# GpSimd's quarter of the low weights from the eleventh z unit on, in place of from the fourth xbc unit on

## The chip, the core and the metric

One NeuronCore of a Trainium2 chip runs the whole program. Five engines work beside each other and meet only at semaphores: TensorE (PE, with its weight loads shown as PEld), VectorE (DVE), ScalarE (ACT), GpSimd (POOL) and SyncE (SP), which here only issues DMAs. The metric is the device time of one execution in microseconds (us), less is better. The kernel before takes 1279.44 us (median of 3 runs, 1279.43 to 1281.62).

## The reference

Two decoder layers on 256 tokens of width 1024, all in float32. Each layer is a half-weighted SwiGLU, a token mixer, a cross attention to 256 memory tokens and a second SwiGLU. The mixer of layer 0 is a short gated convolution, that of layer 1 is a Mamba-2 mixer (SSD). The change lies in the SSD mixer:

```python
z, xbc, dt = jnp.split(h @ w_in, [D_INNER, D_INNER + SSD_CONV_DIM], axis=-1)   # 2048, 4096, 32 columns
xbc = jax.nn.silu(_causal_depthwise_conv(xbc, conv_kernel) + conv_bias)
xs, bm, cm = jnp.split(xbc, [D_INNER, D_INNER + SSD_GROUPS * D_STATE], axis=-1)
dt = jax.nn.softplus(dt + dt_bias);  da = dt * -jnp.exp(a_log);  a_cum = jnp.cumsum(da, axis=-1)
decay = _segsum_exp(a_cum)              # exp(a_cum[l] - a_cum[s]) for s <= l: 32 heads x 2 chunks x 128 x 128
y_diag = jnp.einsum("bgcls,bgrcls,bcsgrp->bclgrp", cb, decay, xdt)
```

followed by the carried state, the gate silu(z), a norm by group and the output projection.

## The kernel before, in words

Every float32 product is made of three products of reduced parts. A weight tile is cut into `w_hi`, its value rounded to the fast matmul type, and `w_lo`, the rest; activations likewise.

The weights stream through four slots, one unit of 128x1024 values at a time, and the units are numbered through the whole program: the SSD mixer has one dt unit, 16 z units, 32 xbc units and 16 half units of the output projection. In this text z0 to z15 and xbc0 to xbc31 are these units, so z10 is the eleventh z unit and xbc3 the fourth xbc unit. For each unit

- SP loads it into `raw` (L339), once `w_lo` of the unit four places earlier is made (L336);
- ACT rounds it into `w_hi` (L422, in the profile line L413);
- DVE subtracts: `w_lo = raw - w_hi` (L850, in the profile line L835), and counts `lo_ready`;
- PE multiplies with both. A z unit is twelve matmuls of 512 columns in two halves (`wide_unit`, L1718), where the first half (k = 0) reads columns 0 to 511 of the unit and the second (k = 1) the rest. An xbc unit is 24 matmuls of 256 columns (`unit`, L1468).

For the units in `SHARED` (L311), which is xbc3 to xbc31, DVE makes only the first 768 columns of `w_lo`, and GpSimd the last 256 (L1413), counted by `lo_pool`. PE waits for both counts, and SP for both before it loads the slot again (L338).

The order of each engine is written out by hand. In step s of the z stage (s = 0 to 15) ACT and DVE split unit z(s+3), three units ahead of PE. Between these splits they have other work:

- `normed`: the normalised activations for the xbc stage, eight tiles of 128x256. DVE multiplies two tiles a step in steps 4 to 7 (L1215), ACT rounds one a step in steps 5 to 12 (L656), GpSimd subtracts one behind each (L1407).
- `decay`: from step 7 to step 14 DVE subtracts and clips eight blocks of 128x128 a step (`diffs`, L1184), and ACT takes the exponential a step later in two instructions of 128x512 (L644). The blocks come by eight broadcast DMAs of 512 KB (L373), which SP issues between the loads of the last z units.
- after the last exponential ACT evicts the last z tiles (`evict_z(3)`, L687), and then rounds xbc3 (L694).

In the xbc stage DVE has three multiply-adds of a convolution out of PSUM for each unit.

Of the kernel before, what the change touches and what calls it, by code (L numbers as in the profile page):

```python
# [19 lines left out]
F32 = mybir.dt.float32  # L20
F32R = mybir.dt.float32r
ALU = mybir.AluOpType
# [6 lines left out]
KT = D_MODEL // P  # L29
# [5 lines left out]
GROUPS = 8  # L35
# [9 lines left out]
UNIT_W = KT * P  # L45
DOWN_W = FT // 2 * P
SLOTS = 4
AHEAD = 3
# [43 lines left out]
def trunk(nc, x_t, mem_t, small, w_gu, w_down, w_conv_in, w_conv_out, w_z, w_xbc, w_dt, w_ssd_out,  # L92
          w_q, w_k, w_v, w_o, out_t, rows_d):
    first, uses, n_units = plan()
# [4 lines left out]
    with ExitStack() as ctx:  # L99
# [19 lines left out]
        a_hi, a_lo, a_lo_at = a[:, 0], a[:, 1], a_hi_at + 4 * FT * SEQ  # L119
        raw = sb("raw", [P, SLOTS, DOWN_W])  # L120
        w_hi, w_hi_at = zip(*(sb_at(f"w_hi{s}", [P, DOWN_W], F32R) for s in range(SLOTS)))
        w_lo, w_lo_at = zip(*(sb_at(f"w_lo{s}", [P, DOWN_W], F32R) for s in range(SLOTS)))
# [4 lines left out]
        z = nc.alloc_sbuf_tensor_at("z", [P, 2, D_INNER], F32, offset=mark + (-mark) % 32)  # L127
# [44 lines left out]
        normed = [t[:, i] for t in (t1_all, t2_all, gate_all, xd) for i in range(2)]  # L172
# [25 lines left out]
        hi_ready, lo_ready = sem("hi_ready"), sem("lo_ready")  # L198
# [24 lines left out]
        normed_ready, nhi_ready, nh_ready = sem("normed_ready"), sem("nhi_ready"), sem("nh_ready")  # L223
        conv_begun, xbc_ready, y_added = (sem(n) for n in ("conv_begun", "xbc_ready", "y_added"))
        lo_pool = sem("lo_pool")
# [71 lines left out]
        H_NORMED = 8  # L297
# [10 lines left out]
        LATE, LAST_ROOT = 5, 7  # L308
        MEM_AGAIN = 36
        SHARED_W = UNIT_W - 256  # L310
        SHARED = range(first["xbc"] + AHEAD, first["xbc"] + 4 * GROUPS)  # L311
        TAIL = {"y": {7: 35}, "zs": {7: 36}, "state": {7: 36}, "y_add": {7: 36}, "yo": {6: 34, 7: 36}, "yoff": {6: 35, 7: 37},
                "square": {6: 36, 7: 38}, "root": {6: 37, 7: 38}, "yn": {5: 35, 6: 37, 7: 38}, "yt": {5: 35, 6: 38, 7: 39}, "a_rest": {5: 36, 6: 39, 7: 40}}
        STEADY = {"cb": 4, "xt": 5, "b_nat": 5, "m0": 5, "m1": 6, "xn": 6, "y": 9, "zs": 9, "state": 10, "y_add": 10, "yo": 11,
# [1022 lines left out]
        @block.gpsimd  # L1337
        def _(pool):
            steps = [0]
            chain = [0]  # L1340

            def add_squares(b):

                for k in range(1, adds(b) + 1):
                    pool.wait_ge(sq_ready, KT * b + k + 1)
                    if k > 1:
                        pool.wait_ge(ssq_step, adds_ahead(b) + k - 1)
                    first_term = sq[0] if k == 1 else ssq
                    nc.gpsimd.tensor_tensor(ssq[:, :], first_term[:, :], sq[k % 3][:, :], ALU.add).then_inc(ssq_step, 1)  # L1349

            def mem_square(i):

                pool.wait_ge(mem_step, 2 * i)
                src = mem[:, bass.ds(i - 1, 1), :].rearrange("p a n -> p (a n)")
                nc.gpsimd.tensor_tensor(mem_sq[:, :], src, src, ALU.mult).then_inc(mem_step, 1)
                pool.wait_ge(mem_step, 2 * i + 1)
                nc.gpsimd.tensor_tensor(mem_ssq[:, :], mem_ssq[:, :], mem_sq[:, :], ALU.add).then_inc(mem_step, 1)

            def a_part(j, count, src):
                pool.wait_ge(ahi_ready, count + 1)  # L1360
                nc.gpsimd.tensor_tensor(j(a_lo), src, j(a_hi).bitcast(F32), ALU.subtract).then_inc(a_ready, 1)  # L1361

            def ffn(f):
                for j in range(2):
                    a_part(lambda t, j=j: t[:, j, :], FFN_A[f] + j, t2[j][:, :])
                if f == 0:
                    pool.wait_ge(mem_in, 64)
                    nc.gpsimd.memset(mem_ssq[:, :], 0.0).then_inc(mem_step, 1)
                    nc.gpsimd.memset(mem_sq[:, :], 0.0).then_inc(mem_step, 1)
                for lo, hi in ((1, KT + 1), (KT + 1, FT // 2)):  # L1370
                    with pool.Fori(lo, hi) as i:
                        for q in range(2):
                            a_part(lambda t, q=q: t[:, bass.ds(2 * i + q, 1), :].rearrange("p a n -> p (a n)"),
                                   FFN_A[f] + 2 * i + q, t2[q][:, :])
                        if f == 0 and lo == 1:
                            mem_square(i)
                project_out(f"down{f}")

            def project_out(phase):
                add_squares(OUT_NORM[phase])  # L1380

            def attention(layer):
                for k in range(KT):
                    a_part(lambda t, k=k: t[:, KT + k, :], Q_A[layer] + k, t2[k % 2][:, :])
                project_out(f"o{layer}")

            def inverse_root_y(g):

                def step(ins, done=pool_step):
                    ins.then_inc(done, 1)  # L1390
                    if done is pool_step:
                        chain[0] += 1
                        pool.wait_ge(pool_step, chain[0])
                r, v, w = (t[:, g % 2, :] for t in (rms_y, var_y, root_y))
                step(nc.gpsimd.tensor_scalar(v, sum_y[:, g % 2, :], 1.0 / GW, EPS, ALU.mult, ALU.add))
                step(nc.gpsimd.tensor_scalar(r.bitcast(mybir.dt.int32), v.bitcast(mybir.dt.int32), -0.5, float(0x5f3759df), ALU.mult, ALU.add))
                for i in range(3):
                    step(nc.gpsimd.tensor_tensor(w, v, r, ALU.mult))
                    step(nc.gpsimd.tensor_tensor(w, w, r, ALU.mult))
                    step(nc.gpsimd.tensor_scalar(w, w, -0.5, 1.5, ALU.mult, ALU.add))  # L1400
                    step(nc.gpsimd.tensor_tensor(r, w, r, ALU.mult), rmsy_ready if i == 2 else pool_step)

            def ssd():
                nx = first["xbc"]
                for k in range(KT):
                    pool.wait_ge(nhi_ready, k + 1)
                    nc.gpsimd.tensor_tensor(a_lo[:, H_NORMED + k, :], normed[k], a_hi[:, H_NORMED + k, :].bitcast(F32), ALU.subtract).then_inc(nh_ready, 1)  # L1407
                for t in range(SSD_STEPS):
                    if nx + t + AHEAD in SHARED:
                        n = nx + t + AHEAD  # L1410
                        s = n % SLOTS
                        pool.wait_ge(hi_ready, n + 1)
                        nc.gpsimd.tensor_tensor(w_lo[s][:, SHARED_W:UNIT_W], raw[:, s, SHARED_W:UNIT_W],  # L1413
                                                w_hi[s][:, SHARED_W:UNIT_W].bitcast(F32), ALU.subtract).then_inc(lo_pool, 1)
                    if ("yoff", t) in due and due["yoff", t] < LATE:
                        g = due["yoff", t]
                        pool.wait_ge(yoff_ready, g + 1)
                        pool.wait_ge(y_added, g + 1)
                        nc.gpsimd.tensor_tensor(y[g % 2][:, 1, :], y[g % 2][:, 1, :], y_off, ALU.add).then_inc(ysum_ready, 1)
                        pool.wait_ge(ysum_ready, g + 1)  # L1420
                        pool.wait_ge(zs_ready, g + 1)
                        nc.gpsimd.tensor_tensor(y[g % 2][:, :, :], y[g % 2][:, :, :], zs[:, :, :], ALU.mult).then_inc(y_ready, 1)
                    if ("root", t) in due and due["root", t] < LAST_ROOT:
                        g = due["root", t]
                        pool.wait_ge(ysq_ready, 2 * g + 2)
                        at_least(pool, yn_ready, 2 * (g - 1))
                        inverse_root_y(g)
                project_out("ssd_out")

            add_squares(0)  # L1430
            ffn(0)
            for k in range(KT):
                a_part(lambda t, k=k: t[:, k, :], CONV_A + k, t2[k % 2][:, :])
            project_out("conv_out")
            attention(0)
            ffn(1)
            ffn(2)
            ssd()
            attention(1)
            ffn(3)  # L1440
# [3 lines left out]
        def _(pe):  # L1444
# [273 lines left out]
            def wide_unit(n, outs, k0, l_hi, l_lo, start, stop, ready=None, part=range(2)):  # L1718

                s = n % SLOTS  # L1720
                pe.wait_ge(lo_ready, n + 1)
                for k in part:
                    if ready:
                        pe.wait_ge(ready[0], ready[1] + k0 + k + 1)
                    w = slice(k * 512, k * 512 + 512)
                    for t in range(2):
                        lt = slice(t * P, t * P + P)
                        ins = three(outs[t][:, :], l_hi[:, k0 + k, lt], l_lo[:, k0 + k, lt], w_hi[s][:, w], w_lo[s][:, w],
                                    start and k == 0, stop and k == 1)
                if k == 1:  # L1730
                    ins.then_inc(unit_done, 1)
# [213 lines left out]
```

## Time and profile before

| | |
|---|---|
| median of 3 runs | 1279.44 us (1279.43 to 1281.62) |
| the profiled execution | 1279.97 us, its span 1278.2 us |
| PE busy | 1268.3 us, 99% of the span |
| DVE busy | 991.9 us, 78% |
| ACT busy | 765.8 us, 60% |
| POOL busy | 261.2 us, 20% |
| granted TensorE clock | 0.999 of full speed |

Times inside the program are microseconds from the start of the span. "Busy" counts the time in which an engine has an instruction in work. In the timelines, neighbouring instructions of one kind are merged, with their number behind x; the bracket at a row's end is the idle time of the engine ahead of it and what ended it. The last z units, the decays and the first xbc units lie between 786 and 829 us.

### The profile page before, as it was taken

What the parts mean: (1) busy time and instruction counts of PE and PEld (TensorE: products, weight loads), DVE (VectorE), ACT (ScalarE), POOL (GpSimd) and SP (SyncE); (2) the same over time, 40 slices, a digit from 0 to 9 for tenths busy, and PEclk for the clock granted to TensorE, in tenths of its full rate; (3) what the DMA queues carried; (4) which work ended last, traced back from release to release, by engine and by line L of the source; (5) the groups of instructions that cost most, each with busy time, mean ns of one, the idle gap of its engine ahead of it and who ended that gap; (6) DMA issues with size and microseconds to landing.
All of it is one profiled execution on the core that took longest, in us unless ns stands there. A gap on an engine that the chain in (4) does not pass through costs nothing.

```text
span 1278.2 us, 23174 instructions
## 1 busy us (share of the span) xinstructions
PE 1268.3 (99%) x7882; PEld 1143.7 (89%) x7882; DVE 991.9 (78%) x1573; ACT 765.8 (60%) x1402; POOL 261.2 (20%) x339
## 2 busy tenths in 40 slices
PE   9999999999999999999999999999999999999997
PEld 7888888898899888888888888999999889888887
DVE  6877778897868787768778768989988777787754
ACT  6655654555655556545656456878866656556643
POOL 2433110123001111111111112336521201111111
PEclk9999999999999999999999999999999999999999
DMA  8566645555545556654556647744445554555661
GB/s 281 174 196 196 223 158 171 197 189 169 165 133 181 188 188 203 223 163 158 193 190 213 213 148 260 228 156 143 134 158 173 182 166 143 170 184 193 220 211 47
DMA packets 63093, 232.49 MB, mean 182 GB/s; under 512 B 7024, under 2 KB 8112, under 8 KB 62896
## 3 DMA queue, kind: packets, MB, share of 16 engines
q1 hardware_dynamic: 62224, 229.69, 55.1%
q10 hardware_dynamic: 800, 1.91, 0.4%
q8 instruction: 40, 0.66, 0.2%
q14 instruction: 29, 0.24, 0.1%
HBM read 230.49 MB, written 1.08 MB: 181 GB/s over the span
## 4 chain that ended last, share of the span: by engine, by line
PE 96%; DMA 1%; DVE 1%; ACT 0%; issue 0%; ACTq 0%; DVEq 0%
PE bank L1446 95%; DMA raw<-w_z 1%; DVE w_lo L835 1%; DMA raw<-w_gu 0%; ACT w_hi L413 0%; PE bank L1801 0%; PE bank L1829 0%; PE bank L1638 0%; DVE decay L1184 0%; PE bank L1576 0%; PE bank L1856 0%; DVE t L838 0%; DVE final L1334 0%; PE bank L1787 0%; ACT L680 0%
## 5 line engine op out<-in xcount | busy, mean ns | idle before, releaser
L835 DVE TENSOR_TENSOR w_lo<-raw,w_hi 128x1024 fp32r<-128x1024 f32 (+3 forms) x403 | 520.1, 1293 | 28.7 <-ACT w_hi L413 28.3
L413 ACT ACTIVATE w_hi<-raw 128x1024 fp32r<-128x1024 f32 (+2 forms) x403 | 442.0, 1098 | 90.1 <-PE bank L1446 80.8
L1446 PE MATMUL bank<-h,w_hi 128*128 128x512 f32 x1744 | 425.7, 391 | 1.4 <-DVE h L838 1.3
L1446 PE MATMUL bank<-a,w_hi 128*128 128x256 f32 (+1 forms) x1878 | 381.6, 324 | 0.4 <-DVE w_lo L835 0.2
L1446 PEld LDWEIGHTS bank<-h,w_hi 128*128 128x128 f32 x1744 | 317.7, 188 | 62.0 <-DVE h L838 2.1
L1446 PEld LDWEIGHTS bank<-a,w_hi 128*128 128x128 f32 x1878 | 312.5, 190 | 26.3 <-issue 0.5
L1446 PE MATMUL bank<-a,w_lo 128*128 128x256 f32 x1280 | 256.4, 283 | 0.0
L1446 PEld LDWEIGHTS bank<-h,w_lo 128*128 128x128 f32 x1736 | 228.5, 191 | 11.2
L1446 PE MATMUL bank<-h,w_lo 128*128 128x256 f32 x1736 | 233.7, 282 | 0.0
L413 ACT ACTIVATE corr<-bank 128x256 f32<-128x256 f32 x263 | 99.0, 377 | 208.3 <-PE bank L1446 208.1
L1446 PEld LDWEIGHTS bank<-a,w_lo 128*128 128x128 f32 x1280 | 201.0, 191 | 2.7
L1361 POOL TENSOR_TENSOR a<-t,a 128x256 f32 (+1 forms) x112 | 102.0, 911 | 492.4 <-ACT a L413 492.4
L835 DVE TENSOR_TENSOR t<-bank,corr 128x256 f32<-128x256 f32 x207 | 86.6, 419 | 88.1 <-ACT corr L413 81.4
L1349 POOL TENSOR_TENSOR ssq<-ssq,sq 128x256 f32<-128x256 f32 x51 | 51.1, 1003 | 181.6 <-ACT sq L446 180.9
L835 DVE TENSOR_TENSOR t<-t,rms 128x256 f32<-128x256 f32 x88 | 72.7, 826 | 3.1
L413 ACT ACTIVATE a<-t 128x256 f32 (+1 forms) x116 | 47.5, 411 | 37.0 <-DVE t L835 37.0
L413 ACT ACTIVATE h<-x,cst 128x256 fp32r<-128x256 f32 x64 | 32.2, 508 | 60.9 <-DVE x L835 60.3
L835 DVE TENSOR_TENSOR acc<-bank,corr 128x256 f32<-128x256 f32 x32 | 13.6, 424 | 67.6 <-ACT corr L413 67.6
L838 DVE SCALAR_TENSOR_TENSOR h<-x,cst,h 128x256 fp32r<-128x256 f32 x64 | 51.3, 806 | 8.0 <-ACT h L413 8.0
L1349 POOL TENSOR_TENSOR ssq<-sq 128x256 f32<-128x256 f32 x9 | 10.2, 1135 | 212.3 <-ACT sq L446 212.3
L838 DVE SCALAR_TENSOR_TENSOR acc<-bank,cst,acc 128x253 f32<-128x253 f32 (+2 forms) x96 | 45.9, 479 | 6.5 <-ACT acc L704 3.8
L835 DVE TENSOR_TENSOR t<-t,gate 128x256 f32<-128x256 f32 (+1 forms) x89 | 38.4, 431 | 10.9 <-ACT gate L466 1.9
(201 smaller groups left out, 1037.6 us busy)
## 6 DMA issues: line engine op xcount, KB each, us to landing
raw<-w_gu SPq DMA_DIRECT2D x174, 512.0 KB, 3.6
raw<-w_down SPq DMA_DIRECT2D x64, 704.0 KB, 4.3
raw<-w_xbc SPq DMA_DIRECT2D x32, 512.0 KB, 4.3
raw<-w_conv_in SPq DMA_DIRECT2D x24, 512.0 KB, 3.5
raw<-w_q SPq DMA_DIRECT2D x16, 512.0 KB, 3.8
raw<-w_k SPq DMA_DIRECT2D x16, 512.0 KB, 3.4
raw<-w_v SPq DMA_DIRECT2D x16, 512.0 KB, 3.5
raw<-w_o SPq DMA_DIRECT2D x16, 512.0 KB, 4.0
```

The costliest lines, as they stand in the source:

```text
L413: return nc.scalar.activation(out, in_, ACT.Copy, scale=scale)
L835: return nc.vector.tensor_tensor(out, a, b, op)
L838: return nc.vector.scalar_tensor_tensor(out=out, in0=a, scalar=scalar, in1=b, op0=op0, op1=op1)
L1349: nc.gpsimd.tensor_tensor(ssq[:, :], first_term[:, :], sq[k % 3][:, :], ALU.add).then_inc(ssq_step, 1)
L1361: nc.gpsimd.tensor_tensor(j(a_lo), src, j(a_hi).bitcast(F32), ALU.subtract).then_inc(a_ready, 1)
L1446: return nc.tensor.matmul(out, lhs, rhs, start=start, stop=stop, skip_group_check=check)
```

## The change

The range `SHARED` begins nine units earlier, at z10: GpSimd now makes columns 768 to 1023 of `w_lo` for z10 to z15 and xbc0 to xbc2 as well, and DVE only columns 0 to 767 of these. GpSimd's code puts the part of unit z(s+3) ahead of its `normed` subtraction of step s. PE waits for `lo_pool` in a shared z unit ahead of the second half only, and in xbc0 to xbc2 ahead of the unit; SP waits for `lo_pool` too before it loads the units four places behind these nine.

```diff
@@ -308,7 +308,8 @@
         SHARED_W = UNIT_W - 256
-        SHARED = range(first["xbc"] + AHEAD, first["xbc"] + 4 * GROUPS)
+        Z_SHARED = 10
+        SHARED = range(first["z"] + Z_SHARED, first["xbc"] + 4 * GROUPS)
@@ -1384,6 +1385,13 @@
+            def low_part(n):
+
+                s = n % SLOTS
+                pool.wait_ge(hi_ready, n + 1)
+                nc.gpsimd.tensor_tensor(w_lo[s][:, SHARED_W:UNIT_W], raw[:, s, SHARED_W:UNIT_W],
+                                        w_hi[s][:, SHARED_W:UNIT_W].bitcast(F32), ALU.subtract).then_inc(lo_pool, 1)
@@ -1401,17 +1409,17 @@
             def ssd():
-                nx = first["xbc"]
-                for k in range(KT):
-                    pool.wait_ge(nhi_ready, k + 1)
-                    nc.gpsimd.tensor_tensor(a_lo[:, H_NORMED + k, :], normed[k], a_hi[:, H_NORMED + k, :].bitcast(F32), ALU.subtract).then_inc(nh_ready, 1)
+                nz, nx = first["z"], first["xbc"]
+                for s in range(5, 16):
+                    if nz + s + AHEAD in SHARED:
+                        low_part(nz + s + AHEAD)
+                    if s < 5 + KT:
+                        k = s - 5
+                        pool.wait_ge(nhi_ready, k + 1)
+                        nc.gpsimd.tensor_tensor(a_lo[:, H_NORMED + k, :], normed[k], a_hi[:, H_NORMED + k, :].bitcast(F32), ALU.subtract).then_inc(nh_ready, 1)
                 for t in range(SSD_STEPS):
                     if nx + t + AHEAD in SHARED:
-                        n = nx + t + AHEAD
-                        s = n % SLOTS
-                        pool.wait_ge(hi_ready, n + 1)
-                        nc.gpsimd.tensor_tensor(w_lo[s][:, SHARED_W:UNIT_W], raw[:, s, SHARED_W:UNIT_W],
-                                                w_hi[s][:, SHARED_W:UNIT_W].bitcast(F32), ALU.subtract).then_inc(lo_pool, 1)
+                        low_part(nx + t + AHEAD)
@@ -1722,6 +1730,8 @@
                 for k in part:
                     if ready:
                         pe.wait_ge(ready[0], ready[1] + k0 + k + 1)
+                    if n in SHARED and k == 1:
+                        pe.wait_ge(lo_pool, n - SHARED[0] + 1)
```

GpSimd's instructions at the start of the SSD mixer, before the change: the eight `normed` subtractions (`a<-t,a`, `a<-gate,a`, `a<-xd,a`), then the shared parts.

```order
L1407 TENSOR_TENSOR a<-t,a 128x256 [waits nhi_ready] x4
L1407 TENSOR_TENSOR a<-gate,a 128x256 [waits nhi_ready] x2
L1407 TENSOR_TENSOR a<-xd,a 128x256 [waits nhi_ready] x2
L1413 TENSOR_TENSOR w_lo<-raw,w_hi 128x256 [waits hi_ready] x13
```

And after the change, at the same place (the code's lines are up to twelve further down):

```order
L1419 TENSOR_TENSOR a<-t,a 128x256 [waits nhi_ready] x2
L1392 TENSOR_TENSOR w_lo<-raw,w_hi 128x256 [waits hi_ready]
L1419 TENSOR_TENSOR a<-t,a 128x256 [waits nhi_ready]
L1392 TENSOR_TENSOR w_lo<-raw,w_hi 128x256 [waits hi_ready]
L1419 TENSOR_TENSOR a<-t,a 128x256 [waits nhi_ready]
L1392 TENSOR_TENSOR w_lo<-raw,w_hi 128x256 [waits hi_ready]
L1419 TENSOR_TENSOR a<-gate,a 128x256 [waits nhi_ready]
L1392 TENSOR_TENSOR w_lo<-raw,w_hi 128x256 [waits hi_ready]
L1419 TENSOR_TENSOR a<-gate,a 128x256 [waits nhi_ready]
L1392 TENSOR_TENSOR w_lo<-raw,w_hi 128x256 [waits hi_ready]
L1419 TENSOR_TENSOR a<-xd,a 128x256 [waits nhi_ready]
L1392 TENSOR_TENSOR w_lo<-raw,w_hi 128x256 [waits hi_ready]
```

Six parts of z10 to z15 now stand between the `normed` subtractions from the third on; those of xbc0 to xbc2 follow behind the last.

PE in the middle of a late z unit, before the change:

```order
L1446 MATMUL bank<-w_hi,h 128x512 [waits lo_ready]
L1446 MATMUL bank<-w_lo,h 128x512
L1446 MATMUL bank<-w_hi,h 128x512 x2
L1446 MATMUL bank<-w_lo,h 128x512
L1446 MATMUL bank<-w_hi,h 128x512 x2
L1446 MATMUL bank<-w_lo,h 128x512
```

and after it, z10:

```order
L1454 MATMUL bank<-w_hi,h 128x512 [waits lo_ready]
L1454 MATMUL bank<-w_lo,h 128x512
L1454 MATMUL bank<-w_hi,h 128x512 x2
L1454 MATMUL bank<-w_lo,h 128x512
L1454 MATMUL bank<-w_hi,h 128x512
L1454 MATMUL bank<-w_hi,h 128x512 [waits lo_pool]
L1454 MATMUL bank<-w_lo,h 128x512
```

The matmuls are the same; the seventh of the unit, the first that reads columns from 512 on, has the wait for GpSimd's part.

## Rows read from the trace of the kernel before

**Rows 1.** The profile's page: busy time, share of the span and instructions.

```profile
PE 1268.3 (99%) x7882; PEld 1143.7 (89%) x7882; DVE 991.9 (78%) x1573; ACT 765.8 (60%) x1402; POOL 261.2 (20%) x339
```

**Rows 2.** Waits of PE's weight loads, 765 to 830 us: total, times, longest.

```profile
PEld bank L1446 <- DVE w_lo L835: 0.7, 1, 0.7
PEld bank L1446 <- issue: 0.5, 1, 0.5
```

**Rows 3.** Timeline of PE: start, length (us), what, count, idle before.

```profile
802.41 0.39 PE L1446 MATMUL bank<-w_hi,h 128*128 128x512 f32 x1
803.03 0.50 PE L1446 MATMUL bank<-w_hi,h 128*128 128x512 f32 x1 [0.24 <-DVE w_lo L835]
...
808.45 0.39 PE L1446 MATMUL bank<-w_hi,h 128*128 128x512 f32 x1
808.98 0.48 PE L1446 MATMUL bank<-a,w_hi 128*128 128x256 f32 x2
...
817.69 0.45 PE L1446 MATMUL bank<-a,w_hi 128*128 128x256 f32 x2
```

**Rows 4.** Timeline of DVE from z10's low part on.

```profile
784.54 0.87 DVE L838 SCALAR_TENSOR_TENSOR gate<-x,cst,rms 128x256 f32<-128x256 f32 x2
787.01 1.23 DVE L835 TENSOR_TENSOR w_lo<-raw,w_hi 128x1024 fp32r<-128x1024 f32 x1 [1.59 <-ACT w_hi L413]
788.15 1.36 DVE L838 SCALAR_TENSOR_TENSOR xd<-x,cst,rms 128x256 f32<-128x256 f32 x2
...
792.14 2.14 DVE L1184 TENSOR_SCALAR decay<-decay,dt_nacum 128x128 f32<-128x128 f32 x8
...
797.97 1.22 DVE L835 TENSOR_TENSOR w_lo<-raw,w_hi 128x1024 fp32r<-128x1024 f32 x1 [0.51 <-ACT w_hi L413]
799.12 2.73 DVE L1184 TENSOR_SCALAR decay<-decay,dt_nacum 128x128 f32<-128x128 f32 x8
...
811.50 1.66 DVE L1184 TENSOR_SCALAR decay<-decay,dt_nacum 128x128 f32<-128x128 f32 x8
813.07 1.21 DVE L835 TENSOR_TENSOR w_lo<-raw,w_hi 128x1024 fp32r<-128x1024 f32 x1
815.96 0.96 DVE L835 TENSOR_TENSOR w_lo<-raw,w_hi 128x768 fp32r<-128x768 f32 x1 [1.67 <-ACT w_hi L413]
816.83 1.51 DVE L838 SCALAR_TENSOR_TENSOR acc<-bank,cst,acc 128x253 f32<-128x253 f32 x3
...
822.00 2.93 DVE L838 SCALAR_TENSOR_TENSOR acc<-bank,cst,acc 128x253 f32<-128x253 f32 x6
```

**Rows 5.** Timeline of POOL over the same stretch.

```profile
791.55 1.27 POOL L1407 TENSOR_TENSOR a<-t,a 128x256 fp32r<-128x256 f32 x1 [2.71 <-ACT a L413]
...
798.33 1.47 POOL L1407 TENSOR_TENSOR a<-gate,a 128x256 fp32r<-128x256 f32 x1 [2.32 <-ACT a L413]
800.96 0.80 POOL L1407 TENSOR_TENSOR a<-xd,a 128x256 fp32r<-128x256 f32 x1 [1.16 <-ACT a L413]
...
816.00 2.21 POOL L1413 TENSOR_TENSOR w_lo<-raw,w_hi 128x256 fp32r<-128x256 f32 x2 [9.72 <-ACT w_hi L413]
...
822.24 0.74 POOL L1413 TENSOR_TENSOR w_lo<-raw,w_hi 128x256 fp32r<-128x256 f32 x1 [0.97 <-ACT w_hi L413]
```

**Rows 6.** Timeline of ACT at the end of the decays.

```profile
813.19 0.64 ACT L644 ACTIVATE decay<-decay 128x512 f32<-128x512 f32 x1 [0.15 <-DVE decay L1184]
813.73 1.25 ACT L413 ACTIVATE z<-bank,rms_n 128x512 f32<-128x512 f32 x2
814.86 1.06 ACT L413 ACTIVATE w_hi<-raw 128x1024 fp32r<-128x1024 f32 x1
```

**Rows 7.** DVE groups from 788 to 815 us: count, busy, mean ns.

```profile
L1184 DVE TENSOR_SCALAR decay<-decay,dt_nacum 128x128 f32<-128x128 f32 x64 | 15.7, 316 | 0.0
```

**Rows 8.** Busy time of each engine in a window, clock, DMA share, GB/s.

```profile
core 0: us, PE busy (x) PEld busy (x) DVE busy (x) ACT busy (x) POOL busy (x), PEclk, DMA share, GB/s
787.00:813.00 26.00, 25.62 (x127) 21.24 (x126) 25.48 (x74) 20.66 (x33) 8.17 (x6) 1.00 0.90 319
```

## What the change does to the time: the prediction

> **What bounds the kernel now.** I read the page's busy shares first, then the waits of PE in the stretch of the change, then the timelines of PE, DVE, POOL and ACT there. PE is busy in 1268.3 of 1278.2 us [rows 1], so what PE does not wait for is worth nothing, and a wait that PE gets is paid in full: no later stage has PE slack in which to lose it. From 765 to 830 us PE's weight loads wait for a low part in two places, 0.7 and 0.5 us [rows 2]; the second is named "issue", but it starts as the first low part of xbc ends. On PE's timeline the loss is smaller. Matmuls of 512 columns normally start 0.23 us apart (a z unit of twelve is 2.75 us), and here the starts are 802.41 and 803.03 us (z14 is late by 0.39) and 808.45 and 808.98 us (xbc0 is late by 0.30) [rows 3]. The most that earlier low parts can give back is 0.69 us.
>
> Both waits are for DVE. In 787 to 813 us it is busy 25.48 of 26 us [rows 8], with one gap of 0.51 us at 797.97 [rows 4]. So the question is whether DVE gets through this stretch sooner, not how much GpSimd could carry (8.17 us busy there).
>
> **What DVE is relieved of.** Where it works without a break, a low part of 1024 columns takes 1.14 us of DVE (787.01 to the next start at 788.15) and one of 768 takes 0.87 (815.96 to 816.83) [rows 4]. Nine units save 0.27 each. Up to the last decay (the start of xbc2's low part, 813.07) eight of them count: 2.16 us.
>
> **What it is charged.** GpSimd gets nine subtractions of 128x256 float32, of the same shape as the eight that it has there. What each of these does to DVE shows in rows 4 and 5. Eight decay subtractions with no GpSimd operation beside them take 1.57 us to the next start (811.50 to 813.07, row length 1.66). The eight at 792.14 have a row of 2.14: GpSimd's operation that began at 791.55 was waiting as DVE's low part ended, went first, and DVE stood for 0.49. The eight at 799.12 have 2.73: two GpSimd operations (798.33 and 800.96), 1.07 together, so the one that began among the decays cost about 0.59. The products at 788.15 take 1.36 against 0.87 at 784.54: 0.49 again. GpSimd pays too: 1.27 and 1.47 us for an operation that takes 0.74 alone (822.24) [rows 5].
>
> Not all DVE work is held up. At 822.00 six multiply-adds that read PSUM take 2.93 us, against 1.51 for three, with a GpSimd part from 822.24 to 822.98 beside them and nothing lost [rows 4, 5]. There the 29 shared parts of before are cheap, since DVE's other work in that stage is of this kind. In the z stage the other work is the decays, from SBUF to SBUF.
>
> So a shared part there takes 0.27 us off DVE and puts 0.49 to 0.59 on. I take 0.54, the middle of the two kinds of meeting. The bounds are 0 (all meet idle time or PSUM work, as at 822.24) and 0.74 (DVE stands for GpSimd's whole operation).
>
> The Trainium skill (SBUF — State Buffer, section Who interferes with whom, with the bullets of SBUF: two separate sides) says that VectorE and GpSimd arbitrate for one port pair by an exclusive lock held for the whole instruction, and that the loser fully blocks. The trace agrees that one of them stands, but prices it at 0.49 to 0.59 and not at the 0.74 of the whole row.
>
> **The sum.** DVE from 787.01 to 813.07 before: eight low parts 9.1; two products 0.87; 64 decays [rows 7], eight times 1.57, 12.6; GpSimd 3.0 (five meetings of 0.49, one of 0.59); the gap 0.51. That is 26.1 and the stretch is 26.06. After: eight low parts 8 x 0.87 = 6.96; products 0.87; decays 12.6; the old meetings 3.0; nine new ones (z10 to z15, xbc0, xbc1, and xbc2, whose `w_hi` is rounded while the last decays run) 9 x 0.54 = 4.86; no gap, since with DVE later z13's `w_hi` is there. That is 28.3, so xbc2's low part starts 2.2 us later, at 815.3.
>
> PE sees it thus. With two GpSimd operations in it, the shared part and a `normed` one, a step costs DVE 0.87 + 1.57 + 0.49 + 0.54 = 3.5 us, while PE is through a z unit in 2.75; in xbc0 and xbc1, with one, it is 2.98 against PE's 2.88 (24 matmuls 0.12 apart). Laid out step by step from 787.01, DVE is ahead of PE up to z12, level at z13, and from z14 on PE waits unit by unit, some 1 us behind today at z14 and 1.5 at xbc0 and xbc1. These are one lag, not several. The last step of it is a chain that today ends in time by less than 0.1 us: last decays (813.07), their exponential on ACT (813.19), the eviction of the last z tiles (813.73), `w_hi` of xbc3 (814.86 to 815.92) [rows 6], its low part on DVE (815.96) and on GpSimd (two parts from 816.00 take 2.21, the second 0.74 of it, so the first is done by about 817.5), PE at 817.69 [rows 3 to 5]. Shifted by 2.2, less the little slack, PE starts xbc3 2.1 us later. PE's two losses of before are inside this number, as it compares places in the span. Behind xbc3 DVE, ACT and PE stand to each other as today, and nothing gives the 2.1 back.
>
> **The waits added.** PE's new wait stands at the seventh matmul of a shared z unit, with the rest of the unit behind it. It ends before PE comes to it: GpSimd begins as soon as `w_hi` is there, while DVE still has decays to do, so `lo_ready`, 1.4 us earlier in PE's order, is last: nothing. On GpSimd the queue behind a shared part is one `normed` subtraction, which PE reads from 809 us on; xbc0 starts at about 810.5 by then and reads the last tile 2.5 us later, when GpSimd is long past it. SP's loads behind z10 to z15 come later with DVE by 0.3 to 1 us. DMA runs at 0.90 of its share in 787 to 813 us [rows 8], so what waits in its queue is not all delayed, and the `w_hi` of z14 to xbc2 have a microsecond between landing and need once DVE is late. Nothing again; if the cover fails it is up to 1 us more.
>
> The profiled execution took 1279.97 us: with 2.1 it would take 1282.1. It lies 0.5 above the median of the runs, 1279.44; on that the forecast is 1281.5.
>
> **The rivals.**
>
> *GpSimd holds DVE longer, or the lag spreads.* At 0.74 a meeting: 9 x 0.74 - 2.16 - 0.51 = 4.0 us, 1283.4. Late slot loads in the full DMA queue would come to about the same. For it: new pairs of GpSimd operations follow each other closely, which today happens once. Against: no meeting in the trace costs over 0.59. The Trainium skill's rule of a block for the whole instruction (SBUF — State Buffer, Who interferes with whom), read by the row's length, is this case.
>
> *The meetings are cheaper.* GpSimd may fall into DVE's idle time ahead of a low part, as at 816.00, where DVE's 768 columns keep their 0.96 and DVE then goes to PSUM work. If a part costs 0.3 to 0.4, DVE is late by 0 to 0.9: 1279.4 to 1280.4. For it: z10 to z12 have real idle time ahead of them (1.59 us at 787.01). Against: from 788 on DVE has work from SBUF without a break, and each meeting there cost 0.49 or more.
>
> *The other side: faster.* DVE comes through sooner, and PE's 0.39 and 0.30 vanish: 1278.8. It decides at a cost of (2.16 + 0.51) / 9 = 0.30 us per shared part; below that the last decay is not later than today. For it: the same sharing is in use from xbc3 on with PE not waiting. Against: that stage has no decays.
>
> That the change does not do what it says is not a case; the instruction order has it.
>
> **How the numbers follow.** A measurement of this kernel can tell 0.2%, 2.6 us, from no change. Forecast (own range +1.3 to +2.8, 1280.7 to 1282.3): 0.60. Longer holds or a spread lag: 0.15. Cheaper meetings: 0.17. Faster: 0.08. Over +2.6 us is a quarter of the first case and nearly all of the second: 0.28. Under -2.6 us there is no mechanism, PE having only 0.69 to win: 0.02. The rest, 0.70, is within 0.2%. For 8 in 10 I leave out most of the faster case and the upper half of the second, and allow for runs that scatter from 1279.4 to 1281.6: 1279.1 to 1283.6.
>
> **What would show it.** Decay rows of eight with 2.6 to 2.8 us where today they have 1.65 to 2.14; `w_lo` of 768 columns, yet xbc2's low part at about 815.3; PE waiting for `w_lo` on nearly each unit from z14 to xbc3; xbc3 at about 819.8 on PE; the same matmuls behind it at a constant distance of 2 us from today. I am wrong if the decay rows keep their length, if PE's waits are for `lo_pool`, or if PE is ahead of today at xbc3.

## The result, and the profile after

The changed kernel takes 1282.38 us, the median of 15 runs (from 1281.67 us), beside 1279.63 us (1279.17 to 1281.62, 15 runs) for the kernel before. The ratio is 1.0021, with a 95% interval of 1.0014 to 1.0028: slower by 2.7 us, between 1.8 and 3.6. One execution of the changed kernel took 2539.88 us, for a reason that no trace shows; ratio and interval leave it out. The profiled execution took 1281.72 us, span 1279.9, against 1279.97 and 1278.2 before: 1.75 us more.

The page's busy line of the changed kernel answers to [rows 1].

```profile
PE 1269.1 (99%) x7882; PEld 1143.8 (89%) x7882; DVE 993.5 (78%) x1573; ACT 766.7 (60%) x1402; POOL 268.5 (21%) x348
```

GpSimd has nine instructions more. DVE, which was relieved of 9 x 256 columns, is busy for 1.6 us longer, not shorter.

The waits of PE's weight loads from 765 to 830 us (answers to [rows 2]):

```profile
PEld bank L1454 <- DVE w_lo L836: 1.3, 2, 0.9
PEld bank L1454 <- issue: 1.1, 2, 0.8
PEld bank L1454 <- ACT z L414: 0.4, 1, 0.4
```

Where there were two waits of 1.2 us in all, there are five of 2.8 (a wait of 0.4 for `corr` is in both and left out here), and one of them is of a kind that was not there: for ACT's eviction of a z tile. None is put down to GpSimd; but the later of the two named "issue", 0.26 us at xbc3, ends as GpSimd's part of xbc3 does (see below).

PE's timeline at the places of [rows 3], and xbc2: the rows are z14, xbc0, xbc2 and xbc3.

```profile
803.38 0.50 PE L1454 MATMUL bank<-w_hi,h 128*128 128x512 f32 x1 [0.46 <-DVE w_lo L836]
...
809.84 0.48 PE L1454 MATMUL bank<-a,w_hi 128*128 128x256 f32 x2 [0.44 <-issue]
...
816.16 0.50 PE L1454 MATMUL bank<-a,w_hi 128*128 128x256 f32 x2 [0.21 <-ACT z L414]
...
819.37 0.48 PE L1454 MATMUL bank<-a,w_hi 128*128 128x256 f32 x2
```

And xbc2 in the kernel before:

```profile
814.81 0.40 PE L1446 MATMUL bank<-a,w_hi 128*128 128x256 f32 x2
```

z14 starts at 803.38 (803.03 before), xbc0 at 809.84 (808.98), xbc2 at 816.16 (814.81), xbc3 at 819.37 (817.69). The lateness grows over the stretch, 0.35, 0.86, 1.35 and at last 1.68 us.

DVE from z10's low part to xbc2's, whole (answers to [rows 4]):

```profile
786.92 0.96 DVE L836 TENSOR_TENSOR w_lo<-raw,w_hi 128x768 fp32r<-128x768 f32 x1 [1.41 <-ACT w_hi L414]
787.80 1.84 DVE L839 SCALAR_TENSOR_TENSOR xd<-x,cst,rms 128x256 f32<-128x256 f32 x2
789.56 2.14 DVE L1185 TENSOR_SCALAR decay<-decay,dt_nacum 128x128 f32<-128x128 f32 x8
791.62 0.95 DVE L836 TENSOR_TENSOR w_lo<-raw,w_hi 128x768 fp32r<-128x768 f32 x1
792.49 3.12 DVE L1185 TENSOR_SCALAR decay<-decay,dt_nacum 128x128 f32<-128x128 f32 x8
795.53 0.95 DVE L836 TENSOR_TENSOR w_lo<-raw,w_hi 128x768 fp32r<-128x768 f32 x1
796.40 1.65 DVE L1185 TENSOR_SCALAR decay<-decay,dt_nacum 128x128 f32<-128x128 f32 x8
797.97 0.94 DVE L836 TENSOR_TENSOR w_lo<-raw,w_hi 128x768 fp32r<-128x768 f32 x1
798.84 3.62 DVE L1185 TENSOR_SCALAR decay<-decay,dt_nacum 128x128 f32<-128x128 f32 x8
802.38 0.95 DVE L836 TENSOR_TENSOR w_lo<-raw,w_hi 128x768 fp32r<-128x768 f32 x1
803.24 2.22 DVE L1185 TENSOR_SCALAR decay<-decay,dt_nacum 128x128 f32<-128x128 f32 x8
805.38 0.95 DVE L836 TENSOR_TENSOR w_lo<-raw,w_hi 128x768 fp32r<-128x768 f32 x1
806.25 2.62 DVE L1185 TENSOR_SCALAR decay<-decay,dt_nacum 128x128 f32<-128x128 f32 x8
808.79 0.95 DVE L836 TENSOR_TENSOR w_lo<-raw,w_hi 128x768 fp32r<-128x768 f32 x1
809.66 2.21 DVE L1185 TENSOR_SCALAR decay<-decay,dt_nacum 128x128 f32<-128x128 f32 x8
811.79 0.95 DVE L836 TENSOR_TENSOR w_lo<-raw,w_hi 128x768 fp32r<-128x768 f32 x1
812.66 2.21 DVE L1185 TENSOR_SCALAR decay<-decay,dt_nacum 128x128 f32<-128x128 f32 x8
814.78 0.95 DVE L836 TENSOR_TENSOR w_lo<-raw,w_hi 128x768 fp32r<-128x768 f32 x1
```

The rows of eight decays are a measure of what GpSimd does to DVE: 1.65 us alone, 2.14 to 2.22 with one GpSimd operation beside them, 2.62 with two, 3.12 with three, 3.62 with four. The four at 798.84 are on GpSimd's own timeline (answers to [rows 5]):

```profile
797.85 1.67 POOL L1392 TENSOR_TENSOR w_lo<-raw,w_hi 128x256 fp32r<-128x256 f32 x1 [2.32 <-ACT w_hi L414]
799.47 0.74 POOL L1419 TENSOR_TENSOR a<-gate,a 128x256 fp32r<-128x256 f32 x1
800.48 0.81 POOL L1392 TENSOR_TENSOR w_lo<-raw,w_hi 128x256 fp32r<-128x256 f32 x1 [0.27 <-ACT w_hi L414]
801.25 0.73 POOL L1419 TENSOR_TENSOR a<-xd,a 128x256 fp32r<-128x256 f32 x1
...
817.71 2.21 POOL L1392 TENSOR_TENSOR w_lo<-raw,w_hi 128x256 fp32r<-128x256 f32 x2 [3.32 <-ACT w_hi L414]
```

The first of them began 0.12 us ahead of DVE's low part of 797.97, stood until that had ended (1.67 instead of 0.74) and then went first. So the engines do not meet only at semaphores, as the first section has it: DVE and GpSimd also stand for each other while both work from SBUF.

The same 64 decays as one group (787 to 816 us; answers to [rows 7]), and the window of [rows 8] with its columns:

```profile
L1185 DVE TENSOR_SCALAR decay<-decay,dt_nacum 128x128 f32<-128x128 f32 x64 | 19.8, 379 | 0.0
```

```profile
787.00:813.00 26.00, 25.10 (x120) 20.32 (x119) 26.00 (x68) 19.55 (x32) 13.57 (x14) 1.00 0.86 318
```

The decays take 19.8 us where they took 15.7. In 787 to 813 us DVE has no idle time at all (26.00 of 26) and ends six instructions behind (68 for 74), PE seven behind (120 for 127). The granted clock is full, as before.

ACT behind the last decay (answers to [rows 6]):

```profile
814.90 0.63 ACT L645 ACTIVATE decay<-decay 128x512 f32<-128x512 f32 x1 [0.71 <-DVE decay L1185]
815.43 1.25 ACT L414 ACTIVATE z<-bank,rms_n 128x512 f32<-128x512 f32 x2
```

and the pieces of the chain that ended last, in order of time (start, us, what):

```profile
812.74 2.14 DVE decay L1185 x8
...
814.90 0.03 ACT decay L645
...
815.43 0.68 ACT z L414
...
816.16 3.13 PE bank L1454 x24
```

The last decays let ACT begin their exponential; the eviction of the last z tiles stands in ACT's queue behind it, and frees the bank that xbc2's matmuls write. From 786.92 to 814.87 the chain is DVE's alone. Behind the 24 matmuls of xbc2 PE stands once more: the first of GpSimd's two parts from 817.71 (2.21 us in all, the second 0.74 of it) ends at about 819.2, and xbc3 starts at 819.37. The kernel before has this wait in its code too, but there the part ends in time.

### The profile page after: what moved, and what is told of

It is laid out like the page before. It is cut to its first block, busy times and chain, and to the rows that moved or that the text cites. A ratio compares the mean times of both kernels' runs of the same rounds, so it can differ in the third digit from the quotient of the medians.

```text
span 1279.9 us, 23193 instructions
## 1 busy us (share of the span) xinstructions
PE 1269.1 (99%) x7882; PEld 1143.8 (89%) x7882; DVE 993.5 (78%) x1573; ACT 766.7 (60%) x1402; POOL 268.5 (21%) x348
## 4 chain that ended last, share of the span: by engine, by line
PE 95%; DVE 3%; DMA 1%; ACT 0%; issue 0%; ACTq 0%; DVEq 0%; SPq 0%
PE bank L1454 94%; DVE decay L1185 1%; DVE w_lo L836 1%; DMA raw<-w_z 0%; DMA raw<-w_gu 0%; PE bank L1811 0%; PE bank L1839 0%; PE bank L1646 0%; ACT w_hi L414 0%; PE bank L1584 0%; DVE xd L839 0%; PE bank L1866 0%; DMA rows_d<-rows 0%; DVE final L1335 0%; PE bank L1797 0%
## 5 line engine op out<-in xcount | busy, mean ns | idle before, releaser
L1350 POOL TENSOR_TENSOR ssq<-sq 128x256 f32<-128x256 f32 x9 | 10.2, 1133 | 212.6 <-ACT sq L447 212.6
```

## The experiments

**How they are compared.** The whole time scatters by more than the effects (see the last section), so each trace is also read over places in it: the distance on PE from the first matmul of z10 to those of z14, xbc0 and xbc3, and from xbc3 to the last matmul; and on DVE from the start of z10's low part to that of xbc2's. "Ops" is the number of full-width GpSimd subtractions in DVE's stretch. The last column is a sum: the stretch, less its gaps, less 8 low parts (1.14 us each of 1024 columns, 0.87 of 768), 0.87 for the products and 8 x 1.57 for the decays, over the ops. Medians are of timed runs, "one" is a single run; the kernel before stood at 1279.63 beside `after`, 1280.28 beside the first four experiments and 1279.84 beside the next four.

```
trace          median   ratio [95%]               PE z10 to z14, xbc0, xbc3  rest    DVE    gaps  ops  per op
before         1279.63                            11.28  17.23  25.93        453.75  26.06  0.51   6   0.50
before_again   one 1281.86                        10.88  16.58  25.28        453.79  25.55  0      6   0.50
before_third   one 1279.72                        10.88  16.72  25.42        453.74  25.67  0.13   6   0.50
e7             1280.35  1.0006 [0.9997, 1.0015]   10.88  16.72  25.42        453.94  25.67  0.03   6   0.51
after          1282.38  1.0021 [1.0014, 1.0028]   11.51  17.96  27.50        453.81  27.86  0     15   0.50
after_again    1282.49  1.0020 [1.0011, 1.0029]   11.75  18.20  27.73        453.80  27.92  0     15   0.50
after_third    one 1284.41                        11.85  18.30  27.84        453.78  27.91  0     15   0.50
e1             1279.50  0.9990 [0.9981, 0.9999]   10.88  16.74  25.45        453.75  25.23  1.68   6   0.53
e2             1284.49  1.0029 [1.0018, 1.0041]   13.33  20.35  30.22        453.74  30.40  0     15   0.52
e3             1282.09  1.0013 [1.0004, 1.0022]   11.57  17.97  27.51        453.82  27.63  0.40  12   0.50
e4             1281.37  1.0006 [0.9997, 1.0015]   11.40  17.56  27.05        453.85  27.38  0.83   9   0.50
e5             1279.63  0.9998 [0.9989, 1.0007]   10.88  16.32  24.95        453.75  25.03  0.52   4   0.49
e6             1281.81  1.0014 [1.0005, 1.0023]   11.40  18.00  27.19        453.76  27.31  0.28  13   0.51
```

The theory: in this stretch each GpSimd subtraction stops DVE's work between two SBUF tiles for about half a microsecond, twice what 256 columns are worth to it, and PE gets the difference as lateness. The rivals: the added waits and their places, later loads, a cost that hangs on GpSimd's work anywhere.

**The pair again.** No edit: after_again, before_again and after_third, before_third are the two kernels once more.

> The changed kernel once more, beside the kernels of this call. In the one trace PE is 1.62 us later behind xbc3 and 0.02 us later anywhere ahead of z14, while the medians lie 2.75 apart. Theory: the path has only those 1.6 us, and the rest is scatter of single runs (1281.67 to 1284.51): a ratio of 1.0013 to 1.0020, and again all of the shift between z14 and xbc3. Rival (a second cost that the first trace missed, as late loads in some executions): a shift in the trace away from that stretch, and again 2.7 us.

> The kernel before once more, for its trace alone. In the run with nine more operations in the xbc stage, whose z stage is that of before, PE came to xbc0 0.5 us sooner than in the first trace. Theory: the two waits of PE at z14 and xbc0 in the first trace depend on when the slot of z13 landed in that execution, so a second trace has them shorter or not at all, and PE at xbc3 up to 0.6 us sooner. Rival (the waits belong to the kernel): the same waits of 0.39 and 0.30 us.

> As before_again. Theory: PE's place at xbc3 differs by some tenths from trace to trace with the landing of z13. Rival: the same to 0.05 us.

> The changed kernel once more. Theory: DVE has no idle time there, so what scatters is only which decays GpSimd meets: PE at xbc3 1.6 to 2.0 us behind the first trace of before. Rival (something else adds a microsecond in most executions): over 2.5.

The repeats moved the base, not the difference. Between medians it is again 2.65 us in after_again (1282.49 and 1279.84), as its rival had it, but the traces show no second place: from z10 to xbc3 after_again is 1.80 us behind the first trace, and behind xbc3 0.05. Of the four traces with the z stage of before (e7 is one), only the first has z14 0.4 us late. Where it comes from is seen on ACT, of before and then of before_third:

```profile
796.88 1.06 ACT L413 ACTIVATE w_hi<-raw 128x1024 fp32r<-128x1024 f32 x1 [1.76 <-DMA raw<-w_z]
```

```profile
796.66 1.06 ACT L413 ACTIVATE w_hi<-raw 128x1024 fp32r<-128x1024 f32 x1 [1.21 <-DMA raw<-w_z]
```

z13's weights landed 0.22 us sooner in before_third, and DVE came to their low part 0.17 us later, so that a gap of only 0.13 us is left:

```profile
797.76 1.23 DVE L835 TENSOR_TENSOR w_lo<-raw,w_hi 128x1024 fp32r<-128x1024 f32 x1
```

So the gap of 0.51 us [rows 4] belongs to an execution, not to the kernel. Of six traces in which this stage is as before up to z13, before_again has none, e7 0.03, before_third 0.13, and e3, the first and e4 have 0.40, 0.51 and 0.83. From z10 to xbc3 PE needs 25.51 us in the mean of the four traces with the z stage of before, and 27.69 in the three of the changed kernel: 2.2 us more, and behind xbc3 the six traces of the two kernels lie within 0.07.

**e1: everything but the columns.** GpSimd's nine new subtractions take 8 columns each instead of 256; the waits, the order and DVE's 768 columns stay as changed. The other 248 columns of these nine low parts are left out.

```diff
 def low_part(n):
     pool.wait_ge(hi_ready, n + 1)
+    end = SHARED_W + 8 if n < nine else UNIT_W
-    nc.gpsimd.tensor_tensor(w_lo[s][:, SHARED_W:UNIT_W], ...
+    nc.gpsimd.tensor_tensor(w_lo[s][:, SHARED_W:end], ...
```

> The changed kernel, but GpSimd makes only 8 of its 256 columns in the nine units z10 to xbc2 (248 columns of their low parts are left out); every wait and every instruction stays. Theory (GpSimd's operations hold DVE up, 0.50 us for each in the changed kernel): with the holds nearly gone DVE keeps the relief of 0.27 us a unit, its time to the last decay falls by about 2 us against before, PE's waits of 0.39 and 0.30 us vanish and the kernel is 0.3 to 0.7 us faster than before (1279.0). Eight columns may still hold DVE a little, 0.1 us each. Rival (the added waits on PE and SP, or the later slot loads, cost the time): as slow as the changed kernel, 1282.4.

Measured: 25.45 us to xbc3, 2.05 less than in after, and a ratio of 0.9990, against 1.0021. The decays between z13 and z14 on DVE:

```profile
799.52 2.13 DVE L1186 TENSOR_SCALAR decay<-decay,dt_nacum 128x128 f32<-128x128 f32 x8
```

They had 3.62 in after. With the same waits in the same places the loss is gone, so it is in the width of GpSimd's work. DVE has 1.68 us of gaps now, yet PE is not ahead of before_third: one new wait shows, 0.26 us at xbc0, for GpSimd's part. The ratio, whose interval ends at 0.9999, puts e1 a little ahead of the kernel before; its trace does not.

**e2: the operations without the relief.** DVE keeps 1024 columns, and GpSimd makes its nine subtractions as well, into a tile that nobody reads then.

```diff
-w = SHARED_W if n in SHARED else width[n]
+w = SHARED_W if n in SHARED and n >= nine else width[n]
...
+nc.gpsimd.tensor_tensor(padded[:, 0:256], raw[:, s, SHARED_W:UNIT_W], ...
```

> The changed kernel, but DVE makes all 1024 columns of the nine units, and GpSimd's nine operations write the same quarter to a tile that nobody reads. Holds without relief. Theory: nine holds of 0.50 us less the gap of 0.51, DVE is 4.0 us late at the last decay, PE the same at xbc3: 1283.6 on the median of before, 1.2 to 1.9 more than the changed kernel. Rival (waits and loads, not the holds): no more than the changed kernel, 1282.4.

Measured: 30.22 us to xbc3, 4.8 more than before_third and 2.72 more than after. DVE's stretch grew by 4.73 us over before_third for nine operations, 0.53 each, and nothing was taken off. This is more than the 4.0 us expected, since the gap of 0.51 was not there to be used up and the holds came to 0.53 and not 0.50. PE waits at each unit from z12 on, here at z14:

```profile
805.92 0.50 PE L1460 MATMUL bank<-w_hi,h 128*128 128x512 f32 x1 [0.84 <-DVE w_lo L837]
```

The relief is the difference to after: 2.54 us on DVE, 2.16 of it the eight narrower low parts; the rest is that its 15 operations cost 0.52 each and those of after 0.50.

**e3 and e4: fewer units.** The sharing begins at z13 (six units) and at xbc0 (three).

```diff
-Z_SHARED = 10
+Z_SHARED = 13    # e3
+Z_SHARED = 16    # e4
```

> The changed kernel with the range from z13 (six units in place of nine). Theory: five reliefs of 0.27 and six holds of 0.50 are +1.65 at the last decay, behind the gap at z13, which nothing uses up now: nearly as slow as the changed kernel, 1281.2 to 1282.0, since z10 to z12 cost 0.7 and the gap takes 0.5 of that. Rival (cost in proportion to the units): two thirds of the changed kernel's, 1281.4. Not sharp by the time alone; the place of xbc2's low part on DVE (814.6 against 813.07 before) tells.

> The range from xbc0 (three units). Theory: two reliefs of 0.27 and three holds of 0.50, +0.96 at the last decay, so PE is 0.9 later at xbc3: 1280.5. Its two waits of before stay. Rival (the z stage's own waits for GpSimd are what costs): no change from before, 1279.6.

e3 measured 27.51 us to xbc3, beside 27.50 to 27.84 for nine units, and xbc2's low part starts at 814.48 on DVE (814.6 expected). But DVE has a gap ahead of z13 in it, which in after the first three parts fill:

```profile
797.69 0.96 DVE L836 TENSOR_TENSOR w_lo<-raw,w_hi 128x768 fp32r<-128x768 f32 x1 [0.40 <-ACT w_hi L414]
```

As the repeats show, such a gap belongs to the execution. Less its 0.40, DVE's stretch in e3 is 1.7 us longer than in before_again (25.55, no gap), which is the sum of the theory, five reliefs of 0.27 and six holds of 0.50; with nine units it is 2.3 us longer. The medians lie 1.8 us above their base in e3 and 2.7 in after. So the likeness of the two traces is chance, the first three units are free only where such a gap is, and the rival, a cost in proportion to the units, is not excluded.

e4 measured 27.05: three units cost 1.5 us over the usual 25.51, and 1.1 over the first trace. That is more than three times 0.23. Here z13's weights were late by more than in any other trace, a gap of 0.83 us, so part of it is the load's and not the sharing's: less the gap, DVE's stretch is 1.0 us longer than in before_again, and 0.96 was expected. The whole time cannot tell e4 from before.

**e5 and e6: move the operations already there.** The eight `normed` tiles are rounded two to a step in four steps, not one to a step in eight, so that GpSimd's subtractions for them are over by 795.1 us. e5 does this to the kernel before, e6 to the changed one.

```diff
-if 5 <= s < 5 + KT:
-    normed_hi(s - 5)
+for k in range(2 * (s - 5), 2 * (s - 4)) if 5 <= s < 9 else ():
+    normed_hi(k)
...               # e6: the same range in GpSimd's loop
```

> The kernel before, with ACT rounding two normed tiles a step in steps 5 to 8 in place of one a step in steps 5 to 12; GpSimd's subtractions follow and so mostly come ahead of the decays. Nothing is shared earlier. Theory: the meetings of GpSimd with the decays behind 797 us (1.07 and 0.49 us of DVE) go, DVE reaches the last decay about 1.5 us sooner, and PE's 0.39 and 0.30 us vanish: 0.5 to 0.7 us faster than before. Rival (ACT, with 0.4 us more in each of four steps, makes w_hi late): no change or slower.

> The changed kernel with the same move of the normed tiles. Nine shared parts still meet the decays, but of the normed subtractions the four or five that did behind 792 us come earlier. Theory: two of the 1.6 us go, so PE at xbc3 is where it was before, -0.3 to +0.5 us. Rival (the shared parts cost by their waits, whatever DVE does): as slow as the changed kernel.

e5 on DVE behind the last of GpSimd's operations:

```profile
801.63 1.22 DVE L835 TENSOR_TENSOR w_lo<-raw,w_hi 128x1024 fp32r<-128x1024 f32 x1
802.77 1.66 DVE L1184 TENSOR_SCALAR decay<-decay,dt_nacum 128x128 f32<-128x128 f32 x8
804.34 1.22 DVE L835 TENSOR_TENSOR w_lo<-raw,w_hi 128x1024 fp32r<-128x1024 f32 x1
```

A step is 2.71 us and PE's unit 2.72 (10.88 us for four): PE has no wait left and reaches xbc3 in 24.95 us. It shows what the stretch can give at most, 0.56 us from the mean of 25.51 and 0.98 from the first trace, and the timed runs cannot tell it from nothing, where 0.5 to 0.7 was expected.

e6 missed its expectation: 27.19 us to xbc3, 1.7 over 25.51. Its DVE rows say why:

```profile
799.61 0.95 DVE L836 TENSOR_TENSOR w_lo<-raw,w_hi 128x768 fp32r<-128x768 f32 x1
800.48 2.21 DVE L1185 TENSOR_SCALAR decay<-decay,dt_nacum 128x128 f32<-128x128 f32 x8
802.61 0.95 DVE L836 TENSOR_TENSOR w_lo<-raw,w_hi 128x768 fp32r<-128x768 f32 x1
```

I had thought that the shared parts hurt because they came on top of the `normed` ones. But one shared part alone makes a step of 3.00 us, above PE's 2.72, while whole low parts with no GpSimd operation make 2.71. And the `normed` subtractions moved ahead still meet DVE at SBUF work there (one row of eight decays of 3.63). So none of the places tried among the decays is good for the sharing.

**e7: nine more operations in another stage.** To the kernel before, nine more GpSimd subtractions of 256 columns are added behind the shared parts of xbc6 to xbc14, into a tile nobody reads then. The z stage is that of before.

```diff
+if n - nx in range(6, 15):
+    ...
+    nc.gpsimd.tensor_tensor(padded[:, 0:256], x[:, 0, :], x[:, 1, :], ALU.subtract)...
```

> The kernel before, with nine more GpSimd subtractions of 128x256 (from SBUF to a tile that nobody reads) in the xbc stage, one behind each shared part of xbc6 to xbc14, where half of DVE's work reads PSUM and PE has slack. Theory (an operation costs only where it meets DVE work from SBUF to SBUF and PE has no slack): PE at most 0.3 us later, the time as before. Rival (each costs 0.5 us of the path wherever it stands): 4 us slower.

Measured: 453.94 us behind xbc3, 0.19 more than 453.75, for all nine together. The DVE rows of e7 there:

```profile
826.00 1.51 DVE L839 SCALAR_TENSOR_TENSOR acc<-bank,cst,acc 128x253 f32<-128x253 f32 x3
827.42 1.46 DVE L836 TENSOR_TENSOR w_lo<-raw,w_hi 128x768 fp32r<-128x768 f32 x1
```

with GpSimd's operations over the same time:

```profile
826.63 0.74 POOL L1414 TENSOR_TENSOR w_lo<-raw,w_hi 128x256 fp32r<-128x256 f32 x1
827.33 0.74 POOL L1418 TENSOR_TENSOR padded<-x 128x256 f32<-128x256 f32 x1
```

The multiply-adds that read PSUM keep their 1.51 beside the one at 826.63; the low part takes 1.46 instead of 0.95, the usual half microsecond. DVE is held here too, but PE does not wait for it. The rival "half a microsecond wherever GpSimd works" fell twice: not all DVE work is held, and not all that is held is on the path. The Trainium skill (SBUF — State Buffer, Who interferes with whom) names as DVE's side of the lock instructions in a two-port mode or with two SBUF inputs; these rows agree, since the multiply-adds have one of their inputs in PSUM. The decays have a single input, in SBUF, and are held in every trace; that they run in a two-port mode no run shows.

## Why the prediction was right, step by step

The forecast was right, 1281.5 us as the likeliest of its cases, and so was the mechanism. Its 2.1 us stands beside 2.2 us of PE time (three traces against four) and 2.7 [1.8, 3.6] between medians. The 0.5 between these two is not explained; it is within the interval, and no place in the traces shows it. The profiled executions of both kernels scatter by more than that ahead of 25 us (last section). The 2.7 is also just beyond the 2.6 us, 0.2%, that the prediction drew as a line and to whose far side it gave only 0.28. Two terms were off and nearly cancelled, which was luck.

- *DVE bounds the stretch and PE pays in full.* Shown: e1 gives 2.05 of it back, and PE's distance behind xbc3 is 453.74 to 453.85 with or without the change.
- *Relief of 0.27 a unit, 2.16 to xbc2.* Shown: the low part is followed after 0.87 in every step of after, and e2 without it is 2.54 us longer on DVE.
- *Nine meetings at 0.54, 4.86.* Too high: 27.86 less 8 x 0.87, 0.87 and 12.56 leaves 7.47 for 15 operations, 0.50 each, and the nine new ones have 4.4 to 4.5 of it beyond the 3.0 to 3.1 of the six old ones. I took the middle between two kinds of meeting; the kind at 0.49 had five rows to the other's one, and all traces together lie at 0.49 to 0.53. The term was 0.4 to 0.5 too large.
- *The gap of 0.51 would be used up.* Three later traces of the same z stage have 0 to 0.13 of it, so it was no stable part of what the change could win. Subtracting it was wrong by as much as the holds were too large: 4.86 - 2.16 - 0.51 = 2.19, and by the ledger 4.4 - 2.16 = 2.2.
- *xbc2's low part at 815.3, xbc3 at 819.8.* 814.78 and 819.37: against the first trace 1.7 and 1.68 late, since that trace itself was slow, by 0.4 us over the mean of the four.
- *PE a unit's 2.75 us, late by 1 us at z14 and 1.5 at xbc0 and xbc1.* A z unit is 2.72 us, which changes nothing in the sum. The lateness was laid out too early: against the first trace it is 0.35 us at z14, 0.86 at xbc0 and 0.91 at xbc1 (812.84 for 811.93), and the last two stops, at xbc2 and xbc3, bring it to 1.68.
- *The last link.* Right in its order, with one release missed: the eviction at 815.43 also frees the bank for xbc2 (PE's wait of 0.21 at 816.16), so the chain comes to PE there, one unit before the place I had named. The GpSimd part from 817.71 then releases xbc3. These two stops are where PE's lag comes up to DVE's.
- *The waits for GpSimd cost nothing.* In after, none of the nine added waits appears; the one that shows, 0.26 at xbc3, was in the code before. They are not always free: 0.26 at xbc0 in e1 and 0.59 at xbc0 in e6.
- *Later loads cost nothing.* DVE has no gap in after's stretch in which it could wait for one, and e1, with the same order of loads, has no loss.
- *The most that PE could win, 0.69.* Too small: e5, without any wait, is 0.98 us faster than the first trace in this stretch. See the next section but one.
- *Rivals.* Holds of 0.74 fell in every trace; cheaper meetings are true of the xbc stage (e7) and not of this one; "faster" decided at 0.30 a part, and the part costs 0.49 to 0.53.
- *What would show it.* Decay rows of 2.6 to 2.8 were named; seen were 1.65 to 3.62, as GpSimd's operations came in bunches, with the mean of 379 ns for 316 carrying it.

## What to carry to other kernels

Before columns go from DVE to GpSimd, compare per operation what DVE is relieved of (here 0.27 us for 256 float32 columns) with what a GpSimd operation costs it (0.50 us while it works from SBUF, almost nothing while it reads PSUM or has slack). GpSimd's idle share is no argument; the neighbour's rows are. And before a gap in one trace enters a sum, see whether a second execution has it.

## What the runs showed of the hardware

**A stall on PE costs more than its gap.** From z14 to xbc0 the first trace takes 5.95 us and e5, without a wait, 5.44: 0.51 more, of which only 0.30 is the late start of xbc0. In after, the first two matmuls from 803.38 are 0.34 us apart and the next ten 0.233, where those ahead of the stall are 0.227 apart; together some 0.18 us that no wait shows. The granted clock reads 1.00 throughout. Why, no run tells.

**A slower beginning in some executions.** The thirteen profiled executions reach z10 at 791.56 to 794.27 us, whatever the kernel. Up to 1.4 us of that is there when PE begins on the first `h`, at 8.8 to 10.2 us. before_again, after_third and e4's profiled run lose 1.5 more in the forty matmuls behind that, by 19 us. From there to z10 all thirteen keep their distance within 0.06. The windows of 9 to 15 us, of before and of before_again (columns as in [rows 8]):

```profile
9.00:15.00 6.00, 6.00 (x33) 5.12 (x34) 5.24 (x9) 5.98 (x15) 1.95 (x2) 1.00 0.98 348
```

```profile
9.00:15.00 6.00, 5.05 (x19) 4.27 (x20) 5.30 (x10) 6.00 (x13) 1.15 (x1) 0.72 0.97 337
```

In the second PE had stood idle longer, 2.47 us instead of 1.31, for DVE's first `h`, and the clock granted in these 6 us is 0.72 of full speed in the mean, with 19 matmuls for 33. From 11.5 to 14.5 us alone it is 0.50, the lower of its two levels (1.00 in before), and from 15 us on it is 1.00. The three slower executions had PE idle for 2.23 to 2.47 us there, the ten others for 0.66 to 1.53 at a clock of 1.00. Both kernels have it, so it is not the change's, and it is as large as the scatter of the runs. The wait on PE, of before_again:

```profile
9.95 0.90 PE L1446 MATMUL bank<-h,w_hi 128*128 128x512 f32 x2 [2.47 <-DVE h L838]
```
